# Two transformer blocks in one launch: four seams of the program rearranged (attention to output product, two norms, RWKV's first inputs, RWKV to output products)

## The chip, the cores and the metric

The kernel runs on one core of a Trainium2 chip. The metric is the device time of one execution in microseconds (us). One core has these engines: PE (TensorE, matrix products; its weight loads are listed as PEld), DVE (VectorE), ACT (ScalarE), POOL (GpSimd) and SP (SyncE, which here issues DMAs alone). PE's granted clock is given as a share of full speed: 1.00 is 2.4 GHz, 0.50 is 1.2 GHz.

## The reference, cut to what matters

1024 tokens of 1024 features pass through two blocks, all in fp32. These are the parts beside which the changed code lies:

```
# first block
x = x + memory_cross_attention(rmsnorm(x, norm_xa_w), rmsnorm(mem, norm_mem_w), ...)
#   4 heads of 256: q = h @ w_q; p = softmax(q k^T / 16) over 256 memory rows
#   o = p @ v, heads side by side; return o @ w_o
x = x + square(relu(rmsnorm(x, norm_ffn_w) @ w_ff1)) @ w_ff2
x = rmsnorm(x, norm_out_w)                      # y = x * rsqrt(mean(x*x) + 1e-6) * w
# second block
z = rmsnorm_2(x, g_mix) @ w_in                  # fox columns, rwkv columns, gate columns
y_fox  = fox_attention(q, k, v, log_f)          # 512 features
yr     = rwkv7_scan(r, decay, k, v, -kk, kk*a)  # 512 features, a recurrence over the tokens
y_rwkv = (group_norm(yr) * gn_g + gn_b + bonus) * g
merged = sigmoid(z_gate1) * (y_fox @ w_o_fox) + sigmoid(z_gate2) * (y_rwkv @ w_o_rwkv)
x = x + merged @ w_out
x = x + ffn_2(rmsnorm_2(x, g_ffn)); x = x + ple(rmsnorm_2(x, g_ple))
```

## The kernel before, in words

Activations lie with the features on the 128 partitions: a tensor of 1024 features is 8 rows k = 0..7, each 128 x 1024 tokens. Each large product is made in fp32 accuracy from three passes of a faster format: both factors are cut into a high and a low part, and the products high by high, low weight by high, and high weight by low are summed in the same PSUM bank (L436 to L438 in `pe_fm`, L592 to L594 in `pe_first`). An output tile of 128 features x 512 tokens over 8 rows is so 24 matmuls of 128x512. ACT makes a high part by a copy, DVE the low part as raw minus high. For weights these are L389 (`ac_cut`) and L397 (`ve_cut`), on tiles of up to 1 MB that SP loads (L378), two buffers in turn.

`pe_first` computes the first four output tiles of a product step by step over k, 12 matmuls for each k, so that PE can begin when the parts of k = 0 are there. `pe_fm` takes one tile after another.

Code is written once per engine as a Python function, and where several streams of work share an engine they are generators, advanced in turns by `together` in a written order. Engines meet by semaphores. Between phases, `next_phase()` puts a barrier over all engines (`meet()`, which first has SP wait for every DMA under way) and frees all banks and signals.

The places that matter below:

**Memory attention.** Eight units (head, half of the tokens) go through eleven turns: turn r makes the scores of unit r (L2164), the transposes of the probabilities of unit r-2 (L2174) and, for unit r-3, two tiles of probabilities times values (L2185). The first of these is copied from PSUM by DVE (L2219), the second by ACT (L2254), and ACT's queue stores both in DRAM, `xo` (L2258). Behind a barrier ACT's queue loads the 8 rows of `xo` back (L675), ACT makes the highs (L682), DVE the lows (L687), and `pe_first` begins the product with w_xo. Then follow x + product, and the first FFN.

**Two norms.** Between the blocks x is normed twice in a row. ACT squares the 8 rows of x, DVE adds them up (L626); ACT squares x times norm_out_w, DVE adds these up (L2470). PE sums both over the partitions with a matrix of ones, after the third product tile of the stage: `out_rms` (L2426, 2 matmuls of plain fp32) and `mix_rms` (L2431, each half a sum of the gained squares plus eps times the plain ones).

**Gates and RWKV.** Stage a4 makes the second block's input product, its last part being 32 gate tiles beside which the fox attention runs (`fox` streams). Behind a barrier RWKV goes over 8 units of 128 tokens in three overlapping steps, pre, inner and scan. SP loads each unit's inputs, 768 KB of `zr` and 512 KB of `rw_d`. The scan's end for the last unit is: DVE sums (L3433 to L3444), ACT's square and rstd (L3463, L3467, L3469), DVE L3448, four transposes on PE (L3402), the gate product (L3412), DVE L3451, POOL L3488, DVE L3456, store in `y2` (L3495).

**Output products.** Behind a barrier the stage a5 loads all 8 rows of `y2` (0 to 3 fox, 4 to 7 RWKV) as above, makes four tiles with w_o_fox (`tiles[0:4]`), four with w_o_rwkv (`tiles[4:8]`), and so on. DVE multiplies each tile in its bank by its sigmoid gate (L3567), which empties the bank.

Of the kernel before, what the change touches and what calls it, by code (L numbers as in the profile page):

```python
# [10 lines left out]
ALU = mybir.AluOpType  # L11
# [214 lines left out]
def program(nc, D, out, S):  # L226
# [3 lines left out]
    with ExitStack() as ctx:  # L230
# [346 lines left out]
        def pe_first(e, tiles, x, ready, feats=None, side=None, at=None):  # L577
# [3 lines left out]
            ps = [bk.take(t.key, RING) for t in tiles]  # L581
# [3 lines left out]
            for i, k in enumerate(feats or range(nk)):  # L585
# [4 lines left out]
                for n, t in enumerate(tiles):  # L590
# [24 lines left out]
        def ac_square_of(e, q, f, seg, sqb):  # L615
# [4 lines left out]
            e.activation(sqb[(f - 1) % 2] if f else RR, xk(f), ACT.Square).then_inc(*z_sq.up())  # L620
# [1423 lines left out]
        def a2():  # L2044
# [91 lines left out]
            sm = [AF[:, 11 * T + 16 * j:11 * T + 16 * j + 16] for j in range(2)]  # L2136
            asks, UNITS, SCORES, QUERIES = [], 8, (0,), (4, 2, 3)
            TURNED, XO_BANKS = (5, 6), (7,)
            for h in range(4):
                tiles = fm(f"xq{h}", "w_xq", 256 * h, 256)  # L2140
                for hf in range(2):
                    asks.append([t for t in tiles if t.hf == hf])
                    for n, t in enumerate(asks[-1]):
                        t.first, t.last = hf + n == 0, hf + n == 2

            def pe_xa(e, r):
# [30 lines left out]
                if 0 <= u < UNITS:  # L2177
# [3 lines left out]
                    for dv in range(2):  # L2181
# [5 lines left out]
                        i.then_inc(*bk.fill(("xa_o", u, dv)))  # L2187

            def ve_xa(e, r):
# [26 lines left out]
                if 0 <= u < UNITS:  # L2216
                    e.wait_ge(*bk.filled(("xa_o", u, 0)))
                    e.wait_ge(*xo_out[0].at(u - 1))
                    e.tensor_copy(xob[0], bk["xa_o", u, 0]).then_inc(*bk.empty(("xa_o", u, 0)))  # L2219
                u = r - 1  # L2220
                if 0 <= u < UNITS:
# [3 lines left out]
                    e.tensor_tensor(g, g, m[:, 12:16].unsqueeze(2).to_broadcast([128, 4, 256]), ALU.mult).then_inc(*xa_prob.up())  # L2225

            def ac_xa(e, r):
# [36 lines left out]
            next_phase()  # L2264

            xos = abreast_last(fm("xo", "w_xo", 0, 1024))
# [4 lines left out]
            def pe_xo(e):  # L2271
                pe_first(e, xos[:4], hp, llo.at)
# [4 lines left out]
            def ve_xo(e):  # L2277
                ve_parts(e, 8, hp, bufs)
# [1598 lines left out]
```

## Time and profile before

| | |
|---|---|
| three runs | 4253.4, 4267.21, 4269.94 us; median 4267.21 |
| profiled execution | 4255.12 us; span of the trace 4253.6 us; mean granted clock 0.943 |
| PE | 3916.8 us busy, 92% of the span, 33542 matmuls |
| PE's weight loads | 3211.7 us, 76% (they overlap PE) |
| DVE | 2141.3 us, 50% |
| ACT | 1153.0 us, 27% |
| POOL | 329.8 us, 8% |
| chain of work that ended last | PE 20%, DVE 2%, ACT 1%, DMA 1% of the span |

The profile is that of one execution, and its times are measured from the start of its span. "Idle before" in a row is the time in which the engine had nothing to do ahead of this instruction, with what ended it. The clock of a stretch is PE's granted clock in it. PE's busy share is near 1.0 in the FFNs and lower in the mixers and the RWKV stage; in the page's row of 40 slices it is 9 or more in most slices, and 7 to 8 between slices 27 and 31.

### The profile page before, as it was taken

How to read it: one execution, taken by the hardware profiler on the slowest of the kernel's cores; microseconds unless marked ns; L12 is line 12 of the kernel's file. 1: busy time of each engine (PE TensorE's matmuls, PEld its weight loads, DVE VectorE, ACT ScalarE, POOL GpSimd, SP SyncE). 2: the span in 40 equal slices, each digit the busy share in tenths (PEclk: the TensorE clock that was granted, in tenths of full speed). 3: DMA queues.
4: the chain of work that ended last, by engine and by line, in shares of the span. 5: the costliest groups of instructions: out<-in, count | busy, mean ns of one | idle time of the engine just before them, and what ended most of it. 6: DMA issues, size and time to landing. Idle time of an engine off the chain costs nothing. (4 is left out here: it accounts for less than half of the span.)

```text
span 4253.6 us, 75535 instructions
## 1 busy us (share of the span) xinstructions
PE 3916.8 (92%) x33542; PEld 3211.7 (76%) x33542; DVE 2141.3 (50%) x3526; ACT 1153.0 (27%) x1595; POOL 329.8 (8%) x362
## 2 busy tenths in 40 slices
PE   6999969988989999999999899778887999999999
PEld 5888847777858888888798677666666788888877
DVE  4643335554434444444624332555554476666673
ACT  4221234433323212212400322333323321111132
POOL 0001102330000000000000000231311000000000
PEclk8999979998999999999999899787888999999999
DMA  5211120114121111111232312211005211111111
GB/s 180 89 52 58 55 92 10 29 33 142 45 80 55 50 50 50 50 50 44 98 97 97 122 55 86 82 36 45 23 10 171 89 50 40 60 40 50 50 45 65
DMA packets 212888, 278.83 MB, mean 66 GB/s; under 512 B 15548, under 2 KB 170940, under 8 KB 212436
## 3 DMA queue, kind: packets, MB, share of 16 engines
q1 hardware_dynamic: 181040, 201.84, 14.9%
q10 hardware_dynamic: 31524, 72.16, 4.5%
q8 instruction: 266, 4.36, 0.4%
q14 instruction: 58, 0.48, 0.0%
HBM read 215.54 MB, written 58.43 MB: 64 GB/s over the span
## 5 line engine op out<-in xcount | busy, mean ns | idle before, releaser
L436 PE MATMUL ps<-sb_a_h,sb_whi 128*128 128x512 f32 x2784 | 1105.3, 397 | 6.0 <-DVE sb_wlo L397 5.5
L438 PE MATMUL ps<-sb_a_h,sb_whi 128*128 128x512 f32 x2784 | 1089.6, 391 | 0.0
L437 PE MATMUL ps<-sb_a_h,sb_wlo 128*128 128x512 f32 x2784 | 1089.2, 391 | 0.0
L436 PEld LDWEIGHTS ps<-sb_a_h,sb_whi 128*128 128x128 f32 x2784 | 525.6, 189 | 133.1 <-issue 15.8
L437 PEld LDWEIGHTS ps<-sb_a_h,sb_wlo 128*128 128x128 f32 x2784 | 525.7, 189 | 112.2 <-issue 4.5
L438 PEld LDWEIGHTS ps<-sb_a_h,sb_whi 128*128 128x128 f32 x2784 | 525.0, 189 | 112.5
L389 ACT ACTIVATE sb_whi<-sb_wraw 128x2048 fp32r<-128x2048 f32 (+3 forms) x146 | 260.3, 1783 | 825.1 <-PE ps L438 500.4
L397 DVE TENSOR_TENSOR sb_wlo<-sb_wraw,sb_whi 128x2048 fp32r<-128x2048 f32 (+3 forms) x146 | 313.9, 2150 | 238.9 <-ACT sb_whi L389 218.3
L548 DVE TENSOR_TENSOR sb_x<-sb_x,ps 128x512 f32<-128x512 f32 x480 | 313.5, 683 | 216.5 <-PE ps L438 207.6
L436 PE MATMUL ps<-sb_a_g,sb_whi 128*128 128x512 f32 x896 | 349.7, 390 | 10.5 <-DVE sb_x L548 10.5
L438 PE MATMUL ps<-sb_a_g,sb_whi 128*128 128x512 f32 x896 | 348.6, 389 | 0.0
L437 PE MATMUL ps<-sb_a_g,sb_wlo 128*128 128x512 f32 x896 | 348.6, 389 | 0.0
L436 PEld LDWEIGHTS ps<-sb_a_g,sb_whi 128*128 128x128 f32 x896 | 168.2, 188 | 49.3 <-DVE sb_x L548 14.7
L438 PEld LDWEIGHTS ps<-sb_a_g,sb_whi 128*128 128x128 f32 x896 | 168.2, 188 | 35.1
L437 PEld LDWEIGHTS ps<-sb_a_g,sb_wlo 128*128 128x128 f32 x896 | 168.2, 188 | 34.5
L2355 DVE SCALAR_TENSOR_TENSOR sb_a_f<-ps,sb_root 128x512 f32<-128x512 f32 x64 | 44.2, 691 | 142.0 <-PE ps L438 136.4
L3673 DVE TENSOR_TENSOR sb_a_f<-ps,sb_root 128x512 f32<-128x512 f32 x88 | 60.8, 691 | 102.2 <-PE ps L438 96.6
L2379 ACT ACTIVATE sb_a_f<-sb_a_f 128x512 f32<-128x512 f32 x64 | 40.5, 632 | 252.1 <-DVE sb_a_f L2355 252.1
L592 PE MATMUL ps<-sb_a_h,sb_whi 128*128 128x512 f32 x128 | 55.5, 434 | 38.0 <-DVE sb_a_h L687 22.1
L3723 ACT ACTIVATE sb_a_g<-sb_a_f 128x512 fp32r<-128x512 f32 x44 | 27.8, 633 | 225.6 <-DVE sb_a_f L3693 225.6
L2358 DVE TENSOR_TENSOR sb_a_g<-sb_a_f,sb_a_g 128x512 fp32r<-128x512 f32 x64 | 44.3, 692 | 87.2 <-ACT sb_a_g L2383 87.2
L2587 POOL MEMSET sb_a_f<- 128x3078 f32 x1 | 2.7, 2683 | 1067.0 <-DVE sb_a_h L612 1067.0
(524 smaller groups left out, 5797.9 us busy)
## 6 DMA issues: line engine op xcount, KB each, us to landing
sb_wraw<-w_in SPq DMA_DIRECT2D x33, 1024.0 KB, 5.3
sb_wraw<-w_ff SPq DMA_DIRECT2D x32, 1024.0 KB, 5.3
sb_wraw<-w_up SPq DMA_DIRECT2D x22, 1024.0 KB, 5.1
sb_wraw<-w_down SPq DMA_DIRECT2D x11, 1024.0 KB, 5.0
sb_wraw<-w_xkv SPq DMA_DIRECT2D x8, 1024.0 KB, 5.4
sb_wraw<-w_out SPq DMA_DIRECT2D x8, 1024.0 KB, 5.2
gates<-sb_a_f ACTq DMA_DIRECT2D x32, 256.0 KB, 2.0
sb_a_f<-gates SPq DMA_DIRECT2D x32, 256.0 KB, 5.0
```

Source lines behind the costliest of these rows:

```text
L389: e.activation(WH[j % 2][:, 0:m], WR[j % 2][:, 0:m], ACT.Copy).then_inc(s_whi, 1)
L397: e.tensor_tensor(WL[j % 2][:, 0:m], WR[j % 2][:, 0:m], WH[j % 2][:, 0:m].bitcast(F32), ALU.subtract).then_inc(s_wlo, 1)
L436: e.matmul(o, wh[:, k, c], xh[:, sl], start=(k == 0), stop=False)
L437: e.matmul(o, wl[:, k, c], xh[:, sl], start=False, stop=False)
L438: m = e.matmul(o, wh[:, k, c], xl[:, sl], start=False, stop=(k == t.nk - 1))
L548: e.tensor_tensor(o, o, bk[t.key], ALU.add).then_inc(*bk.empty(t.key))
L592: e.matmul(ps[n], wh[:, k, c], xh[:, sl], start=(i == 0), stop=False)
L2355: e.scalar_tensor_tensor(b, bk[t.key], 0.0, RR[:, span(t.hf)], ALU.max, ALU.mult).then_inc(*bk.empty(t.key))
L2358: e.tensor_tensor(lo, b, hi.bitcast(F32), ALU.subtract).then_inc(*ff_lo.up())
L2379: e.activation(b, b, ACT.Square).then_inc(*ff_sq.up())
L3673: e.tensor_tensor(raw[:, 2:514], bk[t.key], RR[:, span(t.hf)], ALU.mult).then_inc(*bk.empty(t.key))
L3723: e.activation(gp(g, t.f)[0][:, t.hf * 512:(t.hf + 1) * 512], a, ACT.Copy).then_inc(*cv_hi.up())
```

## The change

Four places are changed, with no change in what the large products compute.

1. **Memory attention to w_xo.** The barrier and the reload of all rows are gone. SP loads rows 0 to 5 of `xo` once the last query tile is made. Units 6 and 7 (rows 6 and 7) no longer go through DRAM: ACT makes the high part straight from PSUM (L2297 after), DVE the low. The highs of rows 0 and 1 stand in turn 8, of 2 and 3 in turn 9, of 4 and 5 in turn 10. PE begins the first four tiles of the product, in banks 0, 2, 3, 4: steps k = 0, 1 behind turn 9's output products, k = 2, 3 behind turn 10's, the rest after.
2. **Two norms.** In place of two sums of squares of which the second was completed by eps times the first, ACT squares x times sqrt(w^2 + eps), column by column (three tiny instructions at FFN group `up[8]`), for `mix_rms`, and plain x for `out_rms`. PE makes the `mix_rms` sums after the second tile, and the `out_rms` sums after the fifth.
3. **RWKV's first inputs.** SP loads them after the ninth gate tile, into a place outside the streams' buffers, in place of after the barrier.
4. **RWKV to output products.** Rows 0 to 3 of `y2` are loaded within the last scan, and cut there by ACT (L3044 after) and DVE (L3034 after). PE makes the first step (k = 0) of `tiles[0:4]` ahead of the last unit's transposes, steps 1 to 3 behind its gate product, all before the barrier. Behind the barrier only rows 4 to 7 are loaded and cut; `tiles[4:8]` take banks 2 to 5, of which 4 and 5 hold `tiles[0]` and `tiles[1]`.

```
-        def pe_first(e, tiles, x, ready, feats=None, side=None, at=None):
+        def pe_first_steps(e, tiles, x, ready, feats=None, side=None, at=None, ring=None):
...
+                yield
...
+            HIGHS = [0, 1, (6, 0), (6, 1), 2, 3, (7, 0), (7, 1), 4, 5]
...
+                if r == 9:
+                    first_steps.append(pe_first_steps(e, xos[:4], hp, xo_ready, None, None, None, (0, 2, 3, 4)))
+                    bk.spot[RING] = 5
+                if r >= 9:
+                    for _ in range(2):
+                        next(first_steps[0])
...
+                        if u >= 6:
+                            e.wait_ge(*bk.filled(("xa_o", u, dv)))
+                            e.activation(hp(6 + dv)[0][:, span(hf)], bk["xa_o", u, dv], ACT.Copy).then_inc(*lhi.up())
...
-            next_phase()
+            sp_xo(sp)
...
-                ve_parts(e, 8, hp, bufs)
-                ac_parts(e, S["xo"], 8, hp, bufs)
...
-                    if n == 2:
-                        sums(e)
+                    if n == 1:
+                        mix_sums(e)
+                    if n == 4:
+                        out_sums(e)
...
+                    if n == 8:
...
+                        load_first(e)
...
+            def pe_tail(e):
+                yield from rest(TAIL + 2)
+                yield from pe_first_steps(e, o_tiles[:4], hp, llo.at, None, None, None, (4, 5, 6, 7))
...
+            def ac_tail(e):
+                yield from rest(TAIL + 1)
+                e.wait_ge(*bk.filled(("rw_w", 7)))
+                e.wait_ge(*rw_bonus.at(7))
+                for k in range(4):
+                    e.wait_ge(*lp[k].at(0))
+                    e.activation(hp(k)[0], raw(k), ACT.Copy).then_inc(*lhi.up())
+                    if k:
+                        yield
...
-                for a in range(2):
-                    pe_first(e, tiles[4 * a:4 * a + 4], lambda k: hp(4 * a + k), lambda k: llo.at(4 * a + k))
+                pe_first(e, tiles[4:8], lambda k: hp(4 + k), llo.at)
```

ACT's instructions at the end of the memory attention, before (`ps` is PSUM, `sb_a_f` raw rows and buffers, `sb_a_h` the parts, `bank_filled` a signal that PE has finished a bank):

```order
L2248 ACTIVATE sb_a_f<-ps 128x512 [waits bank_filled7,bank_filled5]
L2254 ACTIVATE sb_a_f<-ps 128x512 [waits xkv_out3,bank_filled7]
L2258 DMA xo<-sb_a_f 128x512 [waits bank_emptied7] x2
L2254 ACTIVATE sb_a_f<-ps 128x512 [waits xkv_out3,bank_filled7]
L2258 DMA xo<-sb_a_f 128x512 [waits bank_emptied7] x2
L675 DMA sb_a_f<-xo 128x1024 [waits barrier_Pool_Activation_PE_DVE_SP_release]
L675 DMA sb_a_f<-xo 128x1024 x3
L682 ACTIVATE sb_a_h<-sb_a_f 128x1024 [waits part_in0]
```

The same place after, where `part_in` is the signal of a landed row:

```order
L2293 ACTIVATE sb_a_f<-ps 128x512 [waits xkv_out3,bank_filled7]
L2301 DMA xo<-sb_a_f 128x512 [waits bank_emptied7] x2
L2305 ACTIVATE sb_a_h<-sb_b 128x1024 [waits part_in0]
L2305 ACTIVATE sb_a_h<-sb_b 128x1024
L2286 ACTIVATE sb_a_f<-ps 128x512 [waits bank_filled7,bank_filled5]
L2297 ACTIVATE sb_a_h<-ps 128x512 [waits bank_filled7] x2
L2305 ACTIVATE sb_a_h<-sb_b 128x1024 [waits part_in1]
L2305 ACTIVATE sb_a_h<-sb_b 128x1024
L2297 ACTIVATE sb_a_h<-ps 128x512 [waits bank_filled7] x2
L2305 ACTIVATE sb_a_h<-sb_b 128x1024 [waits part_in2]
L2305 ACTIVATE sb_a_h<-sb_b 128x1024
```

The loads have left ACT's queue, and the high parts stand between the copies of the last three units. PE's instructions at the end of the RWKV stage, before (L3393 the last scan product, L3402 transposes, L3412 gate product):

```order
L3393 MATMUL ps<-sb_b 64x64 [waits bank_emptied3]
L3393 MATMUL ps<-sb_b 64x64 x7
L3402 MATMUL ps<-sb_consts,sb_b 128x128 [waits bank_emptied2,rw_out_normed]
L3402 MATMUL ps<-sb_consts,sb_b 128x128 x3
L3412 MATMUL ps<-sb_b 128x128 [waits bank_emptied3,rw_dg3]
L3412 MATMUL ps<-sb_b 128x128 x3
L592 MATMUL ps<-sb_a_h,sb_whi_57 128x512 [waits barrier_Pool_Activation_PE_DVE_SP_release,bank_emptied2,bank_emptied3,bank_emptied1,part_low,bank_emptied0,weights_low_part]
L593 MATMUL ps<-sb_a_h,sb_wlo_59 128x512
```

And after (L3526, L3535 and L3545 are the same three; `part_low` is the signal of a low part):

```order
L3526 MATMUL ps<-sb_b 64x64 [waits bank_emptied3]
L3526 MATMUL ps<-sb_b 64x64 x7
L592 MATMUL ps<-sb_a_h,sb_whi_57 128x512 [waits bank_emptied6,bank_emptied7,bank_emptied5,part_low,bank_emptied4,weights_low_part]
L593 MATMUL ps<-sb_a_h,sb_wlo_59 128x512
L594 MATMUL ps<-sb_a_h,sb_whi_57 128x512
L592 MATMUL ps<-sb_a_h,sb_whi_57 128x512
...
L594 MATMUL ps<-sb_a_h,sb_whi_57 128x512
L3535 MATMUL ps<-sb_consts,sb_b 128x128 [waits bank_emptied2,rw_out_normed]
L3535 MATMUL ps<-sb_consts,sb_b 128x128 x3
L3545 MATMUL ps<-sb_b 128x128 [waits bank_emptied3,rw_dg3]
L3545 MATMUL ps<-sb_b 128x128 x3
L592 MATMUL ps<-sb_a_h,sb_whi_57 128x512 [waits part_low]
...
L592 MATMUL ps<-sb_a_h,sb_whi_56 128x512 [waits barrier_Pool_Activation_PE_DVE_SP_release,bank_emptied4,bank_emptied5,bank_emptied3,part_low,bank_emptied2,weights_low_part]
```

Twelve output matmuls stand ahead of the transposes, 36 behind the gate product, and the first matmul behind the barrier waits for banks 2 to 5, of which 4 and 5 hold tiles that DVE has yet to read. DVE's instructions there, after (L3581 to L3589 are L3448 to L3456 of before, L3710 is L3567 of before; in the last two rows it reads banks 4 and 5):

```order
L3034 TENSOR_TENSOR sb_a_h<-sb_b,sb_a_h 128x1024 [waits part_high] x2
L3581 TENSOR_TENSOR sb_b<-sb_b 128x512 [waits rw_rstd]
L3034 TENSOR_TENSOR sb_a_h<-sb_b,sb_a_h 128x1024 [waits part_high]
L3584 TENSOR_TENSOR sb_b<-ps,sb_params 128x512 [waits bank_filled2]
L3589 TENSOR_TENSOR sb_b<-sb_b,ps 128x512 [waits bank_filled3,rw_bonus_added]
L3034 TENSOR_TENSOR sb_a_h<-sb_b,sb_a_h 128x1024 [waits part_high]
L3701 TENSOR_TENSOR sb_a_h<-sb_b,sb_a_h 128x1024 [waits barrier_Pool_Activation_PE_DVE_SP_release,part_high]
L3701 TENSOR_TENSOR sb_a_h<-sb_b,sb_a_h 128x1024 [waits part_high]
L397 TENSOR_TENSOR sb_wlo_58<-sb_wraw_54,sb_whi_56 128x1024 [waits weights_high_part]
L3701 TENSOR_TENSOR sb_a_h<-sb_b,sb_a_h 128x1024 [waits part_high] x2
L3710 TENSOR_TENSOR sb_x<-sb_a_f,ps 128x512 [waits bank_filled4,rw_out_normed]
L3710 TENSOR_TENSOR sb_x<-sb_a_f,ps 128x512 [waits bank_filled5,rw_out_normed]
```

The four lows of the fox rows stand within the last scan, and DVE comes to banks 4 and 5 only behind all lows of the RWKV rows and a weight cut.

## Rows read from the trace of the kernel before

**Rows 1.** Busy time by stretch (PE, PEld, DVE, ACT, POOL, clock, DMA): first FFN.
```profile
1312.00:2058.00 746.00, 746.00 (x3289) 617.18 (x3288) 363.54 (x451) 173.98 (x191) 0.00 (x0) 1.00 0.15 49
```

**Rows 2.** PE's longest waits: us in total, times, longest.
```profile
PE ps L592 <- DVE sb_a_h L687: 22.1, 2, 11.5
```

**Rows 3.** Timeline where the memory attention ends: start, length, engine [idle before].
```profile
1245.71 0.60 ACT L2254 ACTIVATE sb_a_f<-ps 128x512 f32<-128x512 f32 x1 [1.48 <-PE ps L2185]
...
1246.45 1.96 PE L2185 MATMUL ps<-sb_a_f 128*128 128x512 f32 x4
...
1264.77 1.06 ACT L682 ACTIVATE sb_a_h<-sb_a_f 128x1024 fp32r<-128x1024 f32 x1 [7.46 <-DMA sb_a_f<-xo]
1265.86 1.22 DVE L687 TENSOR_TENSOR sb_a_h<-sb_a_f,sb_a_h 128x1024 fp32r<-128x1024 f32 x1 [11.22 <-ACT sb_a_h L682]
...
1267.23 0.77 PE L592 MATMUL ps<-sb_a_h,sb_whi 128*128 128x512 f32 x1 [10.55 <-DVE sb_a_h L687]
```

**Rows 4.** The same timeline of PE further on.
```profile
1272.37 0.39 PE L592 MATMUL ps<-sb_a_h,sb_whi 128*128 128x512 f32 x1
...
1291.41 0.39 PE L436 MATMUL ps<-sb_a_h,sb_whi 128*128 128x512 f32 x1
```

**Rows 5.** Busy time by stretch around that gap; the clock stands behind POOL.
```profile
1257.00:1262.00 5.00, 0.00 (x0) 0.00 (x0) 0.00 (x0) 0.31 (x1) 0.00 (x0) 1.00 0.51 169
1262.00:1267.00 5.00, 0.00 (x0) 0.00 (x0) 1.14 (x1) 1.06 (x1) 0.00 (x0) 0.50 1.01 374
```

**Rows 6.** Timeline of the two norms' sums, DVE then PE.
```profile
2060.95 9.19 DVE L626 TENSOR_TENSOR sb_root<-sb_root,sb_a_f 128x1024 f32<-128x1024 f32 x7
2070.78 9.20 DVE L2470 TENSOR_TENSOR sb_a_f<-sb_a_f 128x1024 f32<-128x1024 f32 x7 [0.63 <-ACT sb_a_f L2528]
...
2071.10 1.88 PE L2426 MATMUL ps<-sb_root,sb_consts 128*128 128x512 f32 x4
2080.03 2.08 PE L2431 MATMUL ps<-sb_a_f,sb_consts 128*128 128x512 f32 x2 [7.05 <-DVE sb_a_f L2470]
...
2085.41 0.79 PE L436 MATMUL ps<-sb_a_h,sb_whi 128*128 128x512 f32 x1
```

**Rows 7.** Timeline of DVE where the gates have ended.
```profile
2659.80 0.69 DVE L2743 COPY sb_x<-ps 128x512 f32<-128x512 f32 x1 [3.12 <-PE ps L2692]
2663.54 1.23 DVE L3079 TENSOR_TENSOR_SCAN sb_b<-sb_consts,sb_b 128x512 f32<-128x512 f32 x1 [3.05 <-DMA sb_b<-rw_d]
```

**Rows 8.** Timeline of the last RWKV unit.
```profile
3192.31 0.63 ACT L3463 ACTIVATE sb_b<-sb_b 128x512 f32<-128x512 f32 x1 [14.36 <-DVE sb_b L3440]
...
3192.96 1.28 ACT L3467 ACT_TABLE_LOAD   x1
...
3196.11 0.69 DVE L3448 TENSOR_TENSOR sb_b<-sb_b 128x512 f32<-128x512 f32 x1 [2.44 <-ACT sb_b L3469]
...
3196.86 1.12 PE L3402 MATMUL ps<-sb_consts,sb_b 128*128 128x128 f32 x4 [7.03 <-DVE sb_b L3448]
...
3200.08 0.69 DVE L3456 TENSOR_TENSOR sb_b<-sb_b,ps 128x512 f32<-128x512 f32 x1 [1.38 <-POOL sb_b L3488]
```

**Rows 9.** Timeline behind it, ACT then PE.
```profile
3203.38 2.22 ACTq L675 DMA_DIRECT2D sb_a_f<-y  x4
3208.75 1.06 ACT L682 ACTIVATE sb_a_h<-sb_a_f 128x1024 fp32r<-128x1024 f32 x1 [12.68 <-DMA sb_a_f<-y]
...
3211.21 0.77 PE L592 MATMUL ps<-sb_a_h,sb_whi 128*128 128x512 f32 x1 [11.53 <-DVE sb_a_h L687]
...
3228.43 0.77 PE L592 MATMUL ps<-sb_a_h,sb_whi 128*128 128x512 f32 x1 [4.56 <-DVE sb_x L3567]
...
3240.82 0.39 PE L436 MATMUL ps<-sb_a_h,sb_whi 128*128 128x512 f32 x1
```

**Rows 10.** Busy time by stretch: the last RWKV unit, and the whole RWKV stage.
```profile
3180.00:3203.00 23.00, 11.55 (x140) 10.90 (x140) 8.47 (x15) 3.70 (x5) 1.88 (x2) 0.51 0.04 12
2656.00:3203.00 547.00, 422.71 (x8258) 348.73 (x8258) 297.30 (x649) 181.66 (x300) 139.93 (x141) 0.79 0.13 39
```

More of the change, by code:

```diff
@@ L2271, in pe_xo @@
             def pe_xo(e):
-                pe_first(e, xos[:4], hp, llo.at)
+                for _ in first_steps[0]:
+                    pass
                 for t in xos[4:-4]:
@@ L2598, in sp_a4 @@
                     e.wait_ge(*stored(t.key))
-                for t in gates:
+                for n, t in enumerate(gates):
                     if t.first:
@@ new lines, in ac_tail, with po_tail, sp_tail @@
+            def ac_tail(e):
+                yield from rest(TAIL + 1)
+                e.wait_ge(*bk.filled(("rw_w", 7)))
+                e.wait_ge(*rw_bonus.at(7))
+                for k in range(4):
+                    e.wait_ge(*lp[k].at(0))
+                    e.activation(hp(k)[0], raw(k), ACT.Copy).then_inc(*lhi.up())
+                    if k:
+                        yield
+            def po_tail(e):
+                yield from rest(1)
+            def sp_tail(e):
+                yield from rest(TAIL)
+                e.wait_ge(*bk.filled(("rw_o", 6, 1)))
+                e.wait_ge(*fx_out.last())
+                for k in range(4):
+                    e.dma_start(raw(k), S["y2"][k * 128:(k + 1) * 128, :]).then_inc(*lp[k].up())
+                yield
@@ new lines, in with_tail, with both @@
+            def with_tail(f, tail):
+                def both(e):
+                    yield from f(e)
+                    yield from tail(e)
+                return both
+            fox = [with_tail(f, tail)(e) for f, tail, e in (
+                (pe_fox, pe_tail, pe), (ve_fox, ve_tail, ve), (ac_fox, ac_tail, ac), (po_fox, po_tail, po), (sp_fox, sp_tail, sp))]
+            a4(*fox, lambda e: sp_load_inputs(e, 0))
+            o_tiles = out_tiles()
+            meet()
+            al, bt, kt, c_, kk, sq_, am, M, Ba, Br, G1, Y, XA, XT = (room(512) for _ in range(14))
@@ L3583, in ac_a5 @@
             def ac_a5(e):
-                ac_parts(e, S["y2"], 8, hp, bufs)
+                for k in range(4):
+                    e.wait_ge(*lp[k].at(0))
+                    e.activation(hp(4 + k)[0], raw(4 + k), ACT.Copy).then_inc(*lhi.up())
+                    if k == 1:
+                        ac_cut(e, tiles[0].j + 2)
                 for n, t in enumerate(tiles):
```

178 lines of the change are left out of this document (124 added, 54 removed).

## The prediction

> **What bounds the kernel now.** I read the page's first part, then its slices, then PE's waits, then the timeline around the four changed places. PE is busy 92% of the span, and in the first FFN it is busy for all of a stretch of 746 us, 3289 matmuls at clock 1.00 [rows 1]. That gives the price of product work: 746 / 3289 = 0.227 us for a matmul, 2.72 for a step of 12, 21.8 for four tiles (96). At half clock a step costs twice that: from 1267.23 to 1272.37 the 12 of k = 0 take 5.14 us, 0.428 each [rows 3, 4]. So what a seam can give is the time in which PE makes no product work, plus the slow steps behind it. The waits name the places: two waits for the lows of reloaded rows, 22.1 us together [rows 2]; the norms' sums with 7.05 us idle among them [rows 6]; and 4.56 us later in the output products [rows 9]. Behind three of the four seams stand long stretches that PE bounds, so what is won there carries to the end; the third stands ahead of the RWKV stage, where PE is busy 423 of 547 us [rows 10].
>
> **Place 1, memory attention to w_xo.** Before: the last product of the attention that both versions make alike, unit 6's first, begins at 1246.45, and the first four w_xo tiles end at 1291.41 [rows 3, 4]. Between lie 10.55 us idle (barrier, load, 7.46 us of ACT's wait, one high of 1.06, one low of 1.22 [rows 3]) and one step at half clock. Now the rows 0 to 5 are loaded long before, so no load is waited for. Followed from ACT's copy of unit 5, which ends at 1246.31 [rows 3]:
> - ACT makes two highs, 2 x 1.06, and ends near 1248.8 with queueing. The copy of the transposes follows (0.60), then the high of unit 6's first tile, to 1250.0.
> - DVE makes two lows of 1.22, but its copies for turn 10 stand among them; the low of unit 6's second tile ends near 1251.7. In the bank ring unit 6's second product waits for the low of its first tile, since both use one bank. So PE, done at 1248.4, idles 3.3 us.
> - Products of 1.98, then steps k = 0, 1 (5.4): 1259.1. Unit 7's first product to 1261.1, its high and low in series (0.6 + 0.7) to 1262.4, its second to 1264.4, steps 2 and 3 to 1269.9, four more steps (10.9) to 1280.8.
>
> That is 1291.41 - 1280.8 = 10.6 us of gain. Bounds: 12 if ACT and DVE are a copy faster, 6 if the 3.3 us gap costs the clock for two steps and unit 7's hand-over is late too. Before, in 1257 to 1262 the clock was still 1.00 with PE idle, and in 1262 to 1267 it was 0.50 [rows 5]; so I take the 3.3 us gap at no cost in clock. Had it cost one step, the gain would be 2.7 less.
>
> **Place 2, two norms.** Before: from 2071.10 to 2085.41 PE makes no product tile: 14.3 us, of it 1.88 for two plain fp32 sums, 7.05 idle until DVE has the gained sum, and 5.4 for the second sums, which begin at 2.08 for two matmuls, since the clock fell [rows 6]. DVE's first sum over rows ends at 2060.95 + 9.19 = 2070.14. Now `mix_rms` needs only that one, but it stands one tile earlier (2071.10 - 24 x 0.227 = 2065.7), so PE waits until 2070.3: 4.6 us. Then 1.88, and the `out_rms` sums, after three more tiles (16.3 us, to 2088.5), find theirs long done (DVE ends at 2070.78 + 9.20 = 2079.98): 1.88 more. Together 8.4 in place of 14.3: 5.9 us. The 4.6 us gap can cost a slow stretch behind it as 4.56 us did elsewhere [rows 9]; before, the slow part lay inside the 5.4. I charge 1.2 us: gain 4.7. Bounds 2 (a full step and more slow) and 7. The three tiny ACT instructions and two table loads of 1.28 us [rows 8], 3.5 us in all, fall where ACT is idle behind its cuts in the FFN (ACT is busy 174 of 746 us [rows 1]): no cost; uncovered they would be 3.5.
>
> **Place 3, RWKV's first inputs.** Before, DVE's first scan of unit 0 waits for the load until 2663.54, though its last fox copy is over at 2660.49 [rows 7]: 3.05 us. The load now lies beside gate tiles; in the long stretches of such work and in the RWKV stage the DMA share is 0.15 and 0.13 [rows 1, 10], so it hides there. The barrier's other loads stay. Gain 3.0, bounds 0 (the next load or the barrier is as late) and 5. What is saved stands at the head of a chain through unit 0, so I take it whole.
>
> **Place 4, RWKV to output products.** Before: the last DVE piece ends at 3200.77, the barrier lets go at 3203.38, the first row lands at 3208.75 (5.4 us), PE begins at 3211.21; it makes `tiles[0:4]` and waits 4.56 us more before 3228.43, where `tiles[4:8]` begin; these end at 3240.82, where the next tile starts [rows 9]. After, step by step:
> - ACT's square ends at 3192.94 [rows 8]; now two highs (2 x 1.06) stand ahead of the two table loads, so rstd comes 2.1 us later, and DVE's normed rows at 3198.9 in place of 3196.8.
> - PE's step k = 0 can start when the low of row 0 is there, 3194.0 + 1.23, about 3195.3. The clock there is 0.51 [rows 10], so 12 x 0.428 = 5.1 us, until 3200.4. The transposes, which began at 3196.86 [rows 8], wait for that: 3.5 us late. Everything to `y2`'s last store is 3.2 to 3.5 us later, to about 3204.2.
> - Steps 1 to 3 follow the gate product at about 3203.3; 36 matmuls are 8.2 us at full clock and 15.4 at half. I take 7.5 to 8, until 3211: the clock has had work since 3195. The barrier waits for PE, and opens near 3211.3 in place of 3203.4.
> - The load of row 4, 5.4 us: 3216.7. Then four highs, a cut of weights, the lows (1.22 each), the gates' table load and sigmoids, and DVE's reading of banks 5 and 4, at 0.69 each. PE's first matmul of `tiles[4:8]` waits for these: about 3224.5. `tiles[4:8]` are 4 tiles over 4 rows, 48 matmuls: 10.9 us, and 1.4 for a slow start as before (12.4 from 3228.43 to 3240.82). So 3236.5 against 3240.82.
>
> Gain 4.3. Here the 11.53 and 4.56 us of idle become one of about 13. Bounds: loss of 4, if steps 1 to 3 run at half clock (+7) and the gates are late (+1), and gain of 9, if they run at full clock and the transposes find PE free. For moving the loads from ACT's queue to SP's I charge nothing: with both queues the DMA share at such a seam is 1.01 and 374 GB/s [rows 5], so the engines bound it. The Trainium skill says the same ("Trainium Kernel Development and Optimization", Key Constraints): several issuers save only issue time.
>
> A rule of the Trainium skill speaks against this place: matmuls stay in program order, and only weight loads are pulled ahead ("TensorE: Matmul & The Clock Gate", Step-by-step: what each phase is for). By it the 12 matmuls ahead of the transposes cannot step aside for them, as in the steps above. No row of before shows the two side by side; if they could step aside, the gain would be about 7.8 (3.5 more).
>
> **Sum.** 10.6 + 4.7 + 3.0 + 4.3 = 22.6 us. On the profiled execution's 4255.12 that is 4232.5. The profiled execution is 12.1 us under the median 4267.21, so on the median: 4244.6. The runs spread over 16.5 us, so the base alone is worth some 8 us either way. About 0.5% (21.3 us) is what a measurement of this kernel can tell from no change.
>
> **Rivals.**
> - A, part of it is given back, gain 8 to 17, about 4256. The gaps that remain (3.3, 4.6 and 13 us) each cost a slow step, and place 4 comes to nothing since PE's steps 1 to 3 hold the barrier. For it: each gap of 4.5 us or more in the rows is followed by the longer matmul, 0.77 in place of 0.39 [rows 9]. Against it: place 1 alone gives 8 even then.
> - B, more than the sum, gain 28 to 36, about 4235. Steps 1 to 3 run while the end of the last unit is still under way, the clock stays up across all gaps, and place 2 gives 7. For it: at the four places 10.55 + 14.3 + 3.05 + 11.53 + 4.56 us stand without product work on PE or in wait, 44 in all [rows 3, 6, 7, 9]. Against it: the chain at place 4 has the same loads, highs and gates in series.
> - C, slower. RWKV is the stage where the clock wavers: 0.79 over 547 us, with 0.51 in its last 23 us [rows 10]. If other starting points (place 3) move its small matmuls against the clock so that it stands lower for the whole stage, the 423 us of PE work grow. At 0.69 it would be 423 x (0.79 / 0.69 - 1) = 61 us, about half of it on the path (PE is busy 77% of the stage, and waits the rest): +30 against -22.6, so +8, about 4275. It decides below a clock of 0.71. Against it: 3 us of shift is small against what already varies there.
> - D, one way into A: the wait of `tiles[4:8]` for banks 4 and 5 grows beyond the estimate, because four sigmoids and a weight cut come first. Place 4 then loses 4 in place of giving 4.3, and the whole gives about 14.
>
> **How the numbers follow.** The forecast, gain 17 to 28, has 0.58, of which 0.33 lies beyond 21.3 us. A (with D) 0.23, B 0.12, C 0.07. So faster 0.33 + 0.12 = 0.45, same 0.25 + 0.23 = 0.48, slower 0.07. The bounds of the four places sum to 4 and 33 us of gain, 4263 and 4234; with the base's 8 us on the fast side I give 4226 to 4263, which leaves C out.
>
> **What would show it.** In the profile after: no barrier wait behind the memory attention, and PE's `pe_first` steps between its last products, the first four tiles done 10 us earlier relative to unit 6's first product. Before the norms' first sums one wait of about 4.6 us for DVE's first sum over rows, and no second wait. The DVE wait for `rw_d` gone, with the RWKV stage still about 547 us and its clock near 0.79. At the end of it 12 matmuls of 0.43 us ahead of the transposes, the barrier held by PE until about 11 us behind the gate product's start, and PE's next matmul waiting for DVE's reading of bank 4 or 5. I am wrong if the stage clock differs by more than 0.03, if place 4 costs rather than gives, or if place 1 gives less than 6.

## The result, and the profile after

| | before | after |
|---|---|---|
| median of 5 runs | 4260.84 us (4250.04 to 4269.94) | 4226.90 us (4220.46 to 4236.91) |
| ratio of the runs | | 0.9932, 95% interval 0.9912 to 0.9951 |
| ratio in a second set (7 runs against 12) | | 0.9945, 0.9922 to 0.9968 |
| profiled execution's span | 4253.6 us | 4225.1 us |

The change makes the kernel faster by 29 us (21 to 37) by the first set and 23 us (14 to 33) by the second. This is the page of the changed kernel: span, PE's share, and the clock in 40 slices.

```profile
span 4225.1 us, 75524 instructions
...
PE 3906.4 (92%) x33538; PEld 3200.6 (76%) x33538; DVE 2140.5 (51%) x3526; ACT 1154.2 (27%) x1600; POOL 329.4 (8%) x362
...
PEclk9999979998999999999999899787879999999999
```

PE's share stays at 92%. Its matmul time is 10.4 us less with only four matmuls fewer (33538 for 33542). Those four are fp32 sums of the norms, and all these sums together took 7.8 us before (to the end of each group) and 5.6 after, 2.3 less; the rest goes with the clock, 0.948 for 0.943. To see where the time went, I cut both traces at the same instructions. The columns are microseconds between two of them; the columns "2nd trace" are those of the same two kernels run once more.

| stretch | before | before, 2nd trace | after | after, 2nd trace |
|---|---|---|---|---|
| start to unit 6's first output product | 1246.45 | 1248.43 | 1245.65 | 1242.23 |
| place 1: from there to the first four w_xo tiles | 44.96 | 44.83 | 35.39 | 35.44 |
| first FFN, place 2, to the end of the token shift | 895.23 | 895.36 | 888.84 | 888.84 |
| fox attention, first part | 248.30 | 248.38 | 247.86 | 247.79 |
| fox attention, next part | 63.92 | 63.99 | 61.22 | 61.20 |
| fox attention, rest of gates | 151.55 | 151.55 | 151.30 | 151.49 |
| place 3: to DVE's first RWKV scan | 13.13 | 13.17 | 10.00 | 10.00 |
| RWKV stage, to the last unit's square | 528.77 | 534.43 | 530.01 | 529.48 |
| place 4: from there to the tile behind `tiles[4:8]` | 48.51 | 48.41 | 42.15 | 42.44 |
| rest | 1012.78 | 1013.75 | 1012.68 | 1012.49 |

The first trace of each: 9.6 + 6.4 + 0.4 + 2.7 + 0.3 + 3.1 - 1.2 + 6.4 + 0.1, and 0.8 ahead of all, sum 28.5 us. The four places are 25.5 of them. The second traces lie 40.9 us apart, yet the four places are only 25 us of that again; 6.2 fall before unit 6, where PE's work is the same, and 5.0 in the RWKV stage. So the stretches tell what the change did, and whole spans of single traces do not. The places answer to the rows of before as follows.

Place 1 after (DVE, then PE; against [rows 3, 4]):

```profile
1247.00 2.36 DVE L2263 TENSOR_TENSOR sb_a_h<-sb_b,sb_a_h 128x1024 fp32r<-128x1024 f32 x2 [2.58 <-ACT sb_a_h L2305]
1249.27 0.68 DVE L2242 COPY sb_a_f<-ps 128x512 f32<-128x512 f32 x1
1249.88 0.68 DVE L2253 TENSOR_TENSOR sb_a_h<-ps,sb_a_h 128x512 fp32r<-128x512 f32 x1
...
1245.65 1.96 PE L2207 MATMUL ps<-sb_a_f 128*128 128x512 f32 x4
1250.61 3.40 PE L2207 MATMUL ps<-sb_a_f 128*128 128x512 f32 x4 [3.01 <-DVE sb_a_h L2253]
...
1259.58 1.88 PE L2207 MATMUL ps<-sb_a_f 128*128 128x512 f32 x4
1262.87 1.98 PE L2207 MATMUL ps<-sb_a_f 128*128 128x512 f32 x4 [1.41 <-DVE sb_a_h L2253]
...
1281.04 0.39 PE L436 MATMUL ps<-sb_a_h,sb_whi 128*128 128x512 f32 x1
```

No load is waited for. PE has one gap of 3.01 us before unit 6's second product, and one of 1.41 us in unit 7. The clock falls just behind the first (1.00 until 1251.04, then 0.50 until 1254.45), so that this product takes 3.40 us in place of 1.98. The first four tiles end 35.4 us behind unit 6's first product; before it was 45.0.

Place 2 after (DVE, then PE; against [rows 6]):

```profile
2050.58 9.19 DVE L631 TENSOR_TENSOR sb_root<-sb_root,sb_a_f 128x1024 f32<-128x1024 f32 x7
...
2059.83 3.66 PE L2487 MATMUL ps<-sb_root,sb_consts 128*128 128x512 f32 x4 [4.39 <-DVE sb_root L631]
2062.50 1.24 PE L436 MATMUL ps<-sb_a_h,sb_whi 128*128 128x512 f32 x1
...
2079.72 1.89 PE L2494 MATMUL ps<-sb_a_f,sb_consts 128*128 128x512 f32 x4
2081.04 0.80 PE L436 MATMUL ps<-sb_a_h,sb_whi 128*128 128x512 f32 x1
```

One wait of 4.39 us, for the end of DVE's first sum over rows (2050.58 + 9.19). The first sums and most of the first product matmul behind the gap are at half clock (3.66 in place of 1.89, and 1.24 in place of the 0.80 behind the second sums). The second sums wait for nothing.

Place 3 after (DVE; against [rows 7]): the scan follows the copy at once.

```profile
2639.65 0.69 DVE L2814 COPY sb_x<-ps 128x512 f32<-128x512 f32 x1 [3.13 <-PE ps L2763]
2640.26 1.22 DVE L3212 TENSOR_TENSOR_SCAN sb_b<-sb_consts,sb_b 128x512 f32<-128x512 f32 x1
```

Place 4 after (ACT, DVE, PE, SP, PE; against [rows 8, 9]):

```profile
3170.27 0.63 ACT L3596 ACTIVATE sb_b<-sb_b 128x512 f32<-128x512 f32 x1 [15.19 <-DVE sb_b L3573]
...
3190.98 1.06 ACT L3729 ACTIVATE sb_a_h<-sb_b 128x1024 fp32r<-128x1024 f32 x1 [13.15 <-DMA sb_b<-y]
...
3175.96 0.69 DVE L3581 TENSOR_TENSOR sb_b<-sb_b 128x512 f32<-128x512 f32 x1 [1.72 <-ACT sb_b L3602]
...
3180.28 0.69 DVE L3589 TENSOR_TENSOR sb_b<-sb_b,ps 128x512 f32<-128x512 f32 x1 [1.41 <-POOL sb_b L3621]
...
3173.25 0.76 PE L592 MATMUL ps<-sb_a_h,sb_whi 128*128 128x512 f32 x1 [5.47 <-DVE sb_a_h L3034]
...
3177.43 0.60 PE L3535 MATMUL ps<-sb_consts,sb_b 128*128 128x128 f32 x4
...
3187.41 1.75 SPq L3750 DMA_DIRECT2D sb_b<-y  x4
3189.20 0.47 SPq L378 DMA_DIRECT2D sb_wraw<-w_o_fox  x1
...
3199.67 0.76 PE L592 MATMUL ps<-sb_a_h,sb_whi 128*128 128x512 f32 x1 [12.54 <-DVE sb_x L3710]
...
3212.42 0.39 PE L436 MATMUL ps<-sb_a_h,sb_whi 128*128 128x512 f32 x1
```

The step k = 0 begins at 3173.25 at half clock, the transposes follow at 3177.43, the barrier opens at 3187.41, the first row's high starts 3.57 us later, and PE's next matmul waits 12.54 us for DVE's L3710, the reading of a bank.

### The profile page after: what moved, and what is told of

Same layout as the page of the kernel before. It is cut to its first block and busy times, and to the rows that moved or that the text cites. A ratio compares the mean times of both kernels' runs of the same rounds, so it can differ in the third digit from the quotient of the medians.

```text
span 4225.1 us, 75524 instructions
## 1 busy us (share of the span) xinstructions
PE 3906.4 (92%) x33538; PEld 3200.6 (76%) x33538; DVE 2140.5 (51%) x3526; ACT 1154.2 (27%) x1600; POOL 329.4 (8%) x362
## 5 line engine op out<-in xcount | busy, mean ns | idle before, releaser
L592 PE MATMUL ps<-sb_a_h,sb_whi 128*128 128x512 f32 x128 | 56.2, 439 | 29.3 <-DVE sb_x L3710 12.5
```

The lines of the kernel that those rows point to most:

```text
L592: e.matmul(ps[n], wh[:, k, c], xh[:, sl], start=(i == 0), stop=False)
```

## The experiments

Each edit is made to the changed kernel unless it says otherwise. Most stretches of a trace repeat within 0.1 us where the clock stands the same; those of place 4 and of the RWKV stage do not (see below). The runs of one kernel spread over 12 us and more, so the stretches decide. The kernels were timed on several chips, each set beside the kernel before on the same chip, so whole times are compared by the ratio to before.

**One place undone at a time.** The edits are the hunks of the change for that place, taken back.

```
undo_attention:  barrier and ac_parts/ve_parts between attention and w_xo again
undo_norms:      sums(e) after n == 2 again, with the second completed by eps times the first
undo_rwkv_load:  load_first does nothing; sp_pre(0) issues the load behind the barrier
undo_output:     no tails in the last scan; a5 loads and cuts all 8 rows of y2
```

> Place 1 is undone (barrier and reload between memory attention and w_xo as before), places 2, 3 and 4 stay. Theory (each place gives what its own stretch shows): 9.6 us longer than the changed kernel, near 4236.5; the stretch from unit 6's first product to the end of the first four w_xo tiles is again 45.0 us instead of 35.4; nothing moves in the norms, the fox attention or the output products by more than 1 us except where the clock falls by chance. Rival (places interact: what is won ahead is partly given back later): less than 6 us longer.

> Place 2 is undone (the sums of both norms as before), the rest stays. Theory: the norms' stretch gives 4.9 us and no more; the further 4.9 us that the changed kernel's trace shows between the norms and the end of the fox attention are two stretches at half clock that the trace of before happens to have, so this kernel is 5 us longer than the changed one, near 4232, and does not bring those two slow stretches back as a rule. Rival (the later out_rms sums, or the time at which the fox attention starts, cause the difference): 9 to 10 us longer, near 4237, with PE's clock at 0.5 to 0.6 again in the last transposes ahead of the gate tiles.

> Place 3 is undone (RWKV's first inputs loaded behind the barrier again), the rest stays. Theory: 3.1 us longer, near 4230: DVE waits 3 us for rw_d again and nothing else changes. Rival 1 (the clock, not the load, is what differs): within 1 us. Rival 2 (the early load, which lies just where the slow stretch of the fox attention is gone, keeps something from being late there): 6 to 7 us longer, with PE's clock at half there again.

> Place 4 is undone (all rows of y2 loaded and cut behind the barrier, all output products behind it), the rest stays. Theory: 6.4 us longer, near 4233: the stretch from the last unit's square to the first tile behind tiles[4:8] is again 48.5 us instead of 42.2. Rival (the tail's instructions on ACT, DVE and PE slow the RWKV stage itself, since it was 1.2 us longer in the changed kernel's trace): 5 us longer or less, the RWKV stage back at 528.8 us instead of 530.0.

| kernel | median, runs | ratio to before | place 1 | place 2 stretch | fox, next part | place 3 | RWKV stage | place 4 |
|---|---|---|---|---|---|---|---|---|
| undo_attention | 4244.9, 12 | 0.9960 (0.9941 to 0.9978) | 44.57 | 888.81 | 60.95 | 10.03 | 546.62 | 42.34 |
| undo_norms | 4239.1, 9 | 0.9949 (0.9932 to 0.9967) | 35.40 | 894.87 | 61.20 | 9.99 | 524.48 | 43.90 |
| undo_rwkv_load | 4231.8, 6 | 0.9942 (0.9921 to 0.9964) | 35.41 | 888.83 | 61.22 | 12.83 | 522.78 | 42.86 |
| undo_output | 4244.6, 12 | 0.9969 (0.9953 to 0.9984) | 35.38 | 888.84 | 61.19 | 10.00 | 543.44 | 48.54 |

In the traces each place brings back its own stretch: 9.2, 6.0, 2.8 and 6.4 us (against after; place 4 against 42.15), 24.4 together against 25.5 at once. The other places keep theirs, but for place 4, which is 1.8 us longer in undo_norms and 0.7 in undo_rwkv_load; the clock there is the likely reason, as shown below. The theory of separate places holds in the traces, with one size wrong: I had put 4.9 us on the norms, and it is 6.0. The rival for the norms named 9 to 10 us and a median near 4237; the median is 4239.1, but the stretches give 6.0, and the fox part is at 61.20, without the slow clock that the rival wanted.

Whole times say less. By the ratios the four kernels lie 12, 7, 4 and 16 us above the first set of after, and 6, 2, -1 and 10 us above the second. The stretches (9.2, 6.0, 2.8, 6.4) are within these for all but undo_output, and the intervals, 7 to 9 us to either side, cover that one too.

The RWKV stage of the profiled executions of undo_attention and undo_output is 13 to 17 us longer than in after, which is the clock, as the next rows show. Whether those two kernels draw a slow RWKV stage more often, or these executions happened to, one trace each cannot tell; that stays open.

The RWKV stage in three kernels, one row each of busy time by stretch (PE, PEld, DVE, ACT, POOL, then the clock): undo_rwkv_load, after, undo_attention.

```profile
2652.81:3175.59 522.78, 407.40 (x8234) 333.43 (x8234) 293.50 (x642) 175.42 (x290) 137.50 (x137) 0.82 0.14 41
```

```profile
2640.26:3170.27 530.01, 417.94 (x8235) 342.56 (x8234) 293.05 (x643) 174.71 (x289) 135.74 (x136) 0.80 0.13 39
```

```profile
2651.63:3198.25 546.62, 434.48 (x8235) 358.15 (x8234) 293.62 (x643) 174.80 (x290) 135.54 (x136) 0.77 0.13 38
```

The same 8234 or 8235 matmuls take 407, 418 and 434 us, and DVE's and ACT's busy times are equal within 0.7 us. The clock is 0.82, 0.80, 0.77, the stage 522.8, 530.0, 546.6 us: of 27 us more PE work 24 are in the stage's length.

Place 4 varies with the clock too. From the last unit's square to the transposes, in after and in undo_norms:

```profile
3170.27:3177.42 7.15, 4.17 (x12) 3.33 (x13) 4.25 (x5) 7.09 (x9) 0.00 (x0) 0.59 0.00 0
```

```profile
3176.48:3184.70 8.22, 5.25 (x12) 4.02 (x13) 4.96 (x5) 7.49 (x9) 0.00 (x0) 0.50 0.00 0
```

The 12 matmuls of step k = 0 take 4.17 us where the clock rises among them, and 5.25 where it stays at half. In the six traces with this code and the rows loaded first, the clock rises 5.9, 6.2, 6.2, 6.3, 6.9 and 8.4 us behind the square, and the stretch is 42.15, 42.44, 42.34, 42.43, 42.86 and 43.90 us. No run sets this point by itself, so this is a match and not a test.

**The kernel before and the changed kernel, each a second time.**

> The kernel before, unchanged, for a second trace. Theory: what the first trace of before had between 2434 and 2499 us (63.9 us instead of 61.2 in all four kernels with one place undone) was PE's clock in that one execution; here the stretch is 61.2 us. The norms' stretch is again 895 us, the stretch to the w_xo tiles 44.6 to 45.0, the wait for rw_d 3.1, the output products 48.5. The RWKV stage lies anywhere between 523 and 547 us. Rival (the slow stretch belongs to the kernel before): 63.9 us again.

Measured: one time, 4263.81 us, and the stretches of the table above. The rival was right here: the fox attention's slow part is there again, 63.99 us. These are the rows of two stretches of 4 us in before's first trace: behind the 16 one-column products with which the norms' roots are turned into columns, and in the fox attention.

```profile
2160.00:2164.00 4.00, 4.00 (x24) 4.00 (x24) 2.72 (x3) 0.00 (x0) 0.00 (x0) 0.61 0.16 28
2436.00:2440.00 4.00, 3.57 (x11) 2.80 (x12) 0.80 (x5) 0.88 (x4) 0.87 (x2) 0.52 0.83 261
```

The same places in after:

```profile
2145.00:2149.00 4.00, 4.00 (x36) 4.00 (x35) 2.45 (x3) 0.00 (x0) 0.00 (x0) 1.00 0.23 56
2419.00:2423.00 4.00, 3.78 (x18) 3.15 (x19) 1.28 (x6) 0.88 (x4) 0.89 (x2) 1.00 1.06 334
```

The clock is 0.61 and 0.52 before, 1.00 after. The first is in all three traces with the old norms (before twice, undo_norms: the weight load behind this place comes 24.45 us after the one ahead of it) and in after is not (22.96 us), so 1.5 us of the norms' 6 come from there. The second is in both traces of before and in none of the four kernels with one place undone, but once in a kernel that has all four places (steps_behind, below, 64.19). It belongs to no single place; what brings it is not settled. It is 2.7 of the 28.5 us.

> The changed kernel, unchanged, for a second trace and more times on the same chip as the two below. Theory (only four stretches differ from before, by 9.4, 6.3, 3.0 and about 6 us, together 24 to 25; the rest is the clock of one execution): median 4228 to 4240 with before at 4253 to 4264, ratio 0.9935 to 0.9945; in the trace 35.4, 888.8, 10.0 and 42 to 44 us for the four stretches, while the part ahead of them and the RWKV stage lie up to 10 and 20 us off the first trace. Rival (the gain of 34 us that the first runs showed belongs to the change): ratio 0.992 or less again.

Measured: 4231.73 us (4223.11 to 4253.79, 7 runs), ratio 0.9945 (0.9922 to 0.9968), within the theory; the rival's 0.992 is at the edge of the interval. The four places repeat within 0.3 us; the part ahead of them is 3.4 us shorter, and the RWKV stage 0.5.

**What ends the 12.5 us wait of place 4.** Three edits, apart and together.

```
free_banks:
+                bk.spot[RING] = 0
                 pe_first(e, tiles[4:8], lambda k: hp(4 + k), llo.at)
steps_behind:
-                yield from pe_first_steps(e, o_tiles[:4], hp, llo.at, None, None, None, (4, 5, 6, 7))
+                lows = [llo.at(k) for k in range(4)]
+                o_steps.append(pe_first_steps(e, o_tiles[:4], hp, lows.__getitem__, None, None, None, (4, 5, 6, 7)))
+                next(o_steps[0])
+                yield
...
             def pe_a5(e):
+                for _ in o_steps[0]:
+                    pass
```

> The changed kernel with one edit: tiles[4:8] take banks 0 to 3 in place of 2 to 5, so that PE does not wait for DVE's reading of tiles[0] and tiles[1]. Theory (the 12.5 us wait ends last in the banks): PE then waits for the weights' low part, 8.6 us, and the stretch from the last unit's square to the next tiles is 38.1 us in place of 42.2, 4.0 us less; the whole kernel 4 us shorter. Rival (the lows of the rows, or the weight cut, end as late as the banks): less than 1 us.

Measured: 4233.43 us (6 runs), ratio 0.9933 (0.9918 to 0.9948); the stretch 39.17 us. PE's next matmul:

```profile
3198.99 0.80 PE L592 MATMUL ps<-sb_a_h,sb_whi 128*128 128x512 f32 x1 [8.68 <-DVE sb_wlo L397]
```

It waits 8.68 us for the weights' low part in place of 12.54 for the bank. The wait was as expected (8.6), the gain in the stretch 3.0 to 3.3 against the two traces of after in place of 4.0. The barrier opens 0.4 us later behind the square than in after, and the clock stays at half for 4.8 us of the new work in place of 3.8.

> The changed kernel with one edit: steps k = 1 to 3 of tiles[0:4] stand behind the barrier on PE in place of ahead of it (k = 0 stays ahead of the transposes). Theory (these 36 matmuls hold the barrier for 3.8 us and leave PE nothing to do during the load): the barrier opens 3.8 us earlier, PE makes the steps while the rows land, its wait shrinks from 12.5 to under 3 us, and the stretch is 37.5 to 38.5 us in place of 42.2. Rival (PE's 5 us of idle at the barrier costs it the clock for two steps, and what was won is lost): 41 to 43 us.

Measured: 4235.02 us (6 runs), ratio 0.9940 (0.9922 to 0.9958); the stretch 38.08 us, as the theory had it. SP, PE, ACT, PE:

```profile
3207.33 1.75 SPq L3756 DMA_DIRECT2D sb_b<-y  x4
...
3207.37 0.76 PE L592 MATMUL ps<-sb_a_h,sb_whi 128*128 128x512 f32 x1 [4.61 <-PEq L339]
...
3210.81 1.06 ACT L3735 ACTIVATE sb_a_h<-sb_b 128x1024 fp32r<-128x1024 f32 x1 [9.20 <-DMA sb_b<-y]
...
3219.52 0.47 PE L592 MATMUL ps<-sb_a_h,sb_whi 128*128 128x512 f32 x1 [2.35 <-DVE sb_x L3716]
```

The last unit's square is at 3194.06 here, so the barrier opens 13.3 us behind it, against 17.1 in after: the 36 matmuls held it for 3.9 us. PE's wait shrinks to 2.35 us.

> Both edits. Theory: PE goes from step 3 to tiles[4:8] without a wait, the stretch is 35.5 to 36.5 us, 6 us less than in the changed kernel, and the kernel is about 0.14% shorter than it. Rival (either edit alone already reaches what the lows allow): as steps_behind within 0.5 us.

Measured: 4228.06 us (6 runs), ratio 0.9917 (0.9899 to 0.9935); the stretch 33.87 us, 8.4 less than after's mean of 42.3 and better than the 35.5 to 36.5 expected. It is also more than 3.1 and 4.2 us, the two gains apart. In steps_behind PE's last wait of 2.35 us is followed by a second fall of the clock, of 3.4 us; with free banks neither the wait nor the fall is there, and together they are about the 4.2 us between 38.08 and 33.87 (2.35, and half of 3.4). In whole times none of the three is clear of the changed kernel: the ratios are 0.9933, 0.9940 and 0.9917, those of after 0.9932 and 0.9945.

**Place 1's gaps.**

```
attention_bank:
-                        ps = bk.take(("xa_o", u, dv), XO_BANKS)
+                        ps = bk.take(("xa_o", u, dv), (1,) if u >= 6 and dv else XO_BANKS)
```

> The changed kernel with one edit: the second output tile of the attention's units 6 and 7 goes into bank 1, which the scores have left, in place of bank 7. Theory (the two gaps of 3.0 and 1.4 us in place 1, and the slow product behind the first, come from the one bank both tiles share): PE goes through them without a wait, the stretch from unit 6's first product to the first four w_xo tiles is 29.5 to 30.5 us in place of 35.4. Rival (ACT's two highs and DVE's two lows ahead are what is late, since the first step needs the low of row 0): 33 us or more.

Measured: 4223.02 us (6 runs), ratio 0.9919 (0.9897 to 0.9942); the stretch 28.77 us in place of 35.4. PE:

```profile
1249.82 3.67 PE L2207 MATMUL ps<-sb_a_f 128*128 128x512 f32 x8
1252.93 0.80 PE L592 MATMUL ps<-sb_a_h,sb_whi 128*128 128x512 f32 x1
...
1258.82 3.59 PE L2207 MATMUL ps<-sb_a_f 128*128 128x512 f32 x8
...
1278.59 0.39 PE L436 MATMUL ps<-sb_a_h,sb_whi 128*128 128x512 f32 x1
```

The expected 29.5 to 30.5 was too long. Both products of a unit run as one group of 8 matmuls, and both gaps are gone, with them the fall of the clock. The shared bank was the cause of the gaps; the rival, ACT's highs and DVE's lows, would have left them. Of the 6.6 us 4.4 are the gaps and about 1.7 the clock behind the first.

> Steps 1 to 3 behind the barrier, free banks for tiles[4:8], and bank 1 in the attention. Theory (the places don't touch one another): stretch of place 1 as in the kernel with the bank alone, stretch of place 4 33.9 to 35.5 us; against the changed kernel 13 us less, ratio to before 0.990 to 0.9915. Rival (what is won is lost in the clock of the stages between): ratio as that of the changed kernel.

Measured: 4223.64 us (4210.99 to 4228.35, 6 runs), ratio 0.9910 (0.9888 to 0.9932); the stretches 28.77 and 33.95 us. Against the first trace of after that is 14.8 us less at the two places. It is clearly faster than before. Against the changed kernel (4231.73 on the same chip) the medians lie 8 us apart, in the theory's direction and short of its 13, with overlapping intervals; and it is no faster than attention_bank alone (4223.02).

**Why the first row of place 4 landed early.**

```
weights_ahead:
             def sp_a5(e):
+                sp_load(e, tiles[0].j + 3)
```

> The changed kernel with one edit: behind the barrier of place 4, SP issues the next 512 KB weight load ahead of the four rows of y2, as it was before the change (there the weights came from SP's queue at the same moment as the rows from ACT's). Theory (the first row lands in 3.6 us in place of 5.4 because nothing else is under way ahead of it, not because of the queue): 5 to 5.5 us from the row's issue or the barrier to ACT's first high, and the stretch 1.0 to 1.8 us longer than 42.2 to 42.4. Rival (SP's queue itself is the faster one for such rows): 3.6 us again from the row's issue, and at most 0.5 us (the issue of one load) later from the barrier.

Measured: one time, 4231.71 us; the stretch 45.33 us. SP, then ACT:

```profile
3188.94 0.38 SPq L378 DMA_DIRECT2D sb_wraw<-w_o_fox  x1
3189.38 1.92 SPq L3751 DMA_DIRECT2D sb_b<-y  x4
...
3194.30 1.06 ACT L3729 ACTIVATE sb_a_h<-sb_b 128x1024 fp32r<-128x1024 f32 x1 [15.13 <-DMA sb_b<-y]
```

From the row's issue (3189.38) to ACT's high 4.92 us, from the barrier 5.36, as before the change (3203.38 to 3208.75 [rows 9]), against 3.57 in after. With the rows first the ten traces that load them so have 3.5 to 3.7 us. The old way, rows and weights at the same moment from two queues, is less steady: 5.37 us in before, 5.18 in undo_output, but 4.28 in before_again (rows issued at 3211.22):

```profile
3215.50 1.06 ACT L682 ACTIVATE sb_a_h<-sb_a_f 128x1024 fp32r<-128x1024 f32 x1 [11.59 <-DMA sb_a_f<-y]
```

So the order of the transfers accounts for most of it, on one trace of weights_ahead, and SP's queue by itself is not the faster one. The stretch is 3.0 us longer than in after, more than the 1.0 to 1.8 expected; the six traces with the rows first and the same output code lie between 42.15 and 43.90.

## Why the prediction was right, and where a term was off

The forecast was 22.6 us less on the profiled execution and 4244.6 us on the median then known; measured were 28.5 less between the two profiled executions and 23 to 29 by the ratios. The median of 4226.9 lies 17.7 under the forecast, and only 0.9 us inside the fast end of the range given (4226 to 4263). Of the 17.7, 6.4 are the base (with more runs before stands at 4260.8, not 4267.2), 5.9 the difference of the profiled executions from the sum, and the rest the runs' noise. Of the 5.9, the places give 2.9 (-1.0, +1.7, +0.1, +2.1, so that errors partly cancel), and 3.0 fall elsewhere, 2.7 of them in the fox attention, of which the prediction had nothing. That the sum came so near is in part luck; the mechanism at each place is as forecast, with the sizes below. Of the prediction's own mark for a clear gain, 21.3 us, the first set (29, 21 to 37) is at or beyond it, and the second (23, 14 to 33) does not settle it.

- **Place 1, 10.6 forecast, 9.2 to 9.6 measured.** Gap of 3.3 forecast, 3.01 found, unit 7's 1.4 too. What failed is "I take the 3.3 us gap at no cost in clock": from the product behind it to the third matmul after (1250.61 to 1254.57) 3.96 us passed, in unit 7 (1262.87 to 1265.16) 2.29, so the clock cost 1.7 us. The shorter gap and small gains later gave back 0.6, which leaves the 1.0 missing in the first pair of traces. The row of before from which I argued, clock 1.00 in 1257 to 1262 [rows 5], did not carry over: the clock fell here behind a gap of 3.01 us. (Where the working says that the low of unit 6's second tile ends near 1251.7, the first tile is meant; DVE's low of it is what ended the gap.)
- **Place 2, 4.7 forecast, 6.0 to 6.5 measured.** At the seam itself 4.5 to 5.0 were found, with the wait as worked out (4.39 for 4.6). The slow stretch cost about 1.8 us for 1.2 charged (from the first sum to the second product matmul 3.75 us, behind the second sums 1.96), which shorter sums made up. The other 1.5 us are a fall of the clock 70 us later that only the traces with the old norms have; no step of the prediction had it.
- **Place 3, 3.0 forecast, 2.8 to 3.1 measured.** As forecast.
- **Place 4, 4.3 forecast, 6.0 to 6.4 measured in after's two traces** (down to 4.6 in undo_norms). The transposes start 7.2 us behind the square (8.1 forecast, 4.6 before); the last DVE piece ends 2.2 us late (3.2 to 3.5 forecast), because step 0 reached full clock in its second half and the transposes then ran in 0.60 us in place of 1.12. The barrier opens 17.1 us behind the square; I had 19.0. Where the clock stays at half, in undo_norms, the transposes start at 8.2 us and the gain is 4.6, near the forecast.
- **Place 4, the load.** The other mis-sized term is "the load of row 4, 5.4 us": it took 3.57, and weights_ahead shows why. Barrier and load came 3.7 us early; 1.6 were lost behind them (from the first high to PE's matmul 8.7 for 7.8, and 12.75 for 12.0 in `tiles[4:8]`). The forecast's last step is also 0.3 us short by its own figures: 3224.5 + 10.9 + 1.4 is 3236.8, not 3236.5, and the gain by them 4.0. I had argued that the queue makes no difference, which weights_ahead bears out, but overlooked that SP now issues the rows ahead of the weights. The rule I cited with it, that several issuers save only issue time (the Trainium skill, "Trainium Kernel Development and Optimization", Key Constraints), stands beside that: with two queues the rows and the weights went out at the same moment, with one queue there is an order, worth 0.7 to 1.8 us at the row by the three traces of the old way.
- **The bank wait, 12.5 us**, was named as it came: PE's next matmul waits for DVE's reading. free_banks shows the bank to be worth 3 us, the rest being the barrier and the load.
- **The rule on program order** (the Trainium skill, "TensorE: Matmul & The Clock Gate", Step-by-step: what each phase is for) agrees with the trace: the transposes' input was ready at 3175.96 + 0.69 = 3176.65, and they began behind step 0, at 3177.43. The 12 matmuls cost them 0.8 us here and 1.9 in undo_norms (3182.85 to 3184.71), where the clock stayed at half; the rest of the delay, 1.9 us, is ACT's two highs ahead of its table loads.
- **Rivals.** A (a part given back) didn't come. B (more than the sum) came in part, not for its reason: PE's gaps lost the clock, and the surplus is the load, the earlier barrier, two falls of the clock and the base. C's mechanism exists: the RWKV stage goes from 523 to 547 us with the clock at 0.82 to 0.77, and almost all of it is on the path (24 of 27 us), not half. But its direction is not the change's: 530.0 and 529.5 after, 528.8 and 534.4 before. D (place 4 loses by the bank wait) did not come: that wait is 12.5 us, where the forecast had about 13.

## What to carry to other kernels

A seam is worth what PE does not do in it, plus the slow stretch behind it, and such terms add up when each place is followed by work that PE bounds. When work is drawn ahead of a barrier, ask what then holds the barrier: 36 matmuls ahead of it made the stretch 4.2 us longer than it is with them in the time of the load behind it. Where a wait is long, look for what is second: here the bank, the barrier and the weight cut lay within 4 us of each other, and two edits together gave what neither gave alone.

## What the runs showed of the hardware that was not expected

- The clock fell to half behind an idle gap of PE of 3.01 us (a product of 3.40 in place of 1.98 us), while in before it stood at 1.00 for the first 5 us of a longer one. The stretch around it is 35.4 us in eight of the nine traces with this gap, and 36.72 in one (steps_behind_free_banks), where the clock stays at half for 6.8 us in place of 3.4.
- With a 512 KB weight load issued ahead of it, the first row of 512 KB was used 4.92 us behind its issue (one trace), and 3.5 to 3.7 us with the rows first (ten traces).
- Without any edit in it, a stage of 8234 small matmuls varied by 24 us between traces (522.7 in attention_bank, 546.6 in undo_attention), nearly all of it with the clock; as much as the whole change. The part ahead of unit 6's first product, where PE's work is the same in all, varied from 1242.2 to 1259.6 us.
